# Conditioning vectors of a hybrid decoder step: loaded by input tiles, multiplied 256 columns wide, two more of them in the mixers' waits

## What is computed

```
mod = (silu(c) @ w_ada + b_ada).reshape(B, 9, 1024)      # s1 sc1 g1 s2 sc2 g2 s3 sc3 g3
x = LN(ALPHA*x + 0.5*(1+g1) * swiglu(x*(1+sc1)+s1, ffn1_wgu, ffn1_wdown))
proj = (x*(1+sc2)+s2) @ w_in                             # pooling, RG-LRU and gate inputs
mix  = [pool_mix(u_pool) | gelu(u_gate)*RGLRU(conv(u_lru))] @ w_out
x = LN(ALPHA*x + (1+g2) * mix)
x = LN(ALPHA*x + 0.5*(1+g3) * swiglu(x*(1+sc3)+s3, ffn2_wgu, ffn2_wdown))
```

## Time and profile before

| | |
|---|---|
| median of 3 runs | 1059.66 us (1057.15 to 1059.95) |
| profiled execution | 1059.47 us, of it 1057.5 us span |
| busy share of VectorE, ScalarE, GpSimd | 59%, 43%, 10% |
| moved by the DMA engines | 234.73 MB, mean 222 GB/s |
| conditioning matmuls L511 | 2048 records, mean 274 ns |
| chunks of `ada_raw` | 72 transfers of 1 MiB |

### The profile page before, as it was taken

The page is one execution under the profiler, slowest core; times in us unless marked ns, Lnnn a source line. Parts: engine busy times, 40 slices in busy tenths (PEclk is TensorE's granted clock), DMA queues, the critical chain, the costliest instruction groups (busy, mean ns, idle before and its releaser), DMA issues.

```text
span 1057.5 us, 21707 instructions
## 1 busy us (share of the span) xinstructions
PE 1005.0 (95%) x9548; PEld 970.7 (92%) x9548; DVE 620.1 (59%) x929; ACT 455.3 (43%) x564; POOL 110.5 (10%) x171
## 2 busy tenths in 40 slices
PE   4798999999999999999999999999998989999996
PEld 2598999998988999999989999999897989999995
DVE  1364554457898664544577554455789756555464
ACT  2243443334484444433344444333448445443342
POOL 1420000000510420000006000000060032000000
PEclk9799999999999999999999999999998989999998
DMA  9978898877549679785956998797861627765521
GB/s 302 288 250 235 252 260 299 306 258 235 213 137 275 184 212 273 230 299 176 315 164 216 241 316 238 254 319 255 274 219 51 190 81 205 198 184 158 184 93 42
DMA packets 283329, 234.73 MB, mean 222 GB/s; under 512 B 7328, under 2 KB 249114, under 8 KB 283219
## 3 DMA queue, kind: packets, MB, share of 16 engines
q1 hardware_dynamic: 281136, 229.70, 70.5%
q0 software_dynamic: 1792, 2.54, 0.9%
q10 hardware_dynamic: 306, 1.12, 0.3%
HBM read 232.06 MB, written 1.78 MB: 221 GB/s over the span
## 4 chain that ended last, share of the span: by engine, by line
PE 59%; DVE 7%; DMA 2%; issue 1%; ACT 1%; SPq 0%; DVEq 0%; ACTq 0%
PE bank L485 18%; PE bank L486 18%; PE bank L487 17%; PE bank L511 3%; PE bank L496 2%; DMA raw<-in_ffn_wgu_dram 2%; ACT w_hi L807 1%; DVE w_lo L1019 1%; DVE rstd L1105 1%; DVE xc L1282 1%; DVE z L1095 0%; DVE z L1083 0%; PE bank L692 0%; DVE sq L1109 0%; DVE x L1453 0%
## 5 line engine op out<-in xcount | busy, mean ns | idle before, releaser
L485 PE MATMUL bank<-m_hi,w_hi 128*128 128x264 f32 x1664 | 480.9, 289 | 22.6 <-DVE m_lo L1126 10.7
L486 PE MATMUL bank<-m_lo,w_hi 128*128 128x264 f32 x1664 | 475.9, 286 | 0.0
L487 PE MATMUL bank<-m_hi,w_lo 128*128 128x264 f32 x1664 | 475.1, 286 | 0.0
L1019 DVE TENSOR_TENSOR w_lo<-raw,w_hi 128x2048 fp32r<-128x2048 f32 (+2 forms) x156 | 337.9, 2166 | 223.3 <-ACT w_hi L807 222.7
L807 ACT ACTIVATE w_hi<-raw 128x2048 fp32r<-128x2048 f32 (+2 forms) x156 | 280.1, 1797 | 186.6 <-PE bank L487 165.9
L485 PEld LDWEIGHTS bank<-m_hi,w_hi 128*128 128x128 f32 x1664 | 317.5, 191 | 28.4 <-issue 18.0
L486 PEld LDWEIGHTS bank<-m_lo,w_hi 128*128 128x128 f32 x1664 | 317.8, 191 | 0.1
L487 PEld LDWEIGHTS bank<-m_hi,w_lo 128*128 128x128 f32 x1664 | 316.4, 190 | 0.0
L485 PE MATMUL bank<-h_hi,w_hi 128*128 128x264 f32 x672 | 193.9, 288 | 0.0
L487 PE MATMUL bank<-h_hi,w_lo 128*128 128x264 f32 x672 | 191.0, 284 | 0.0
L486 PE MATMUL bank<-h_lo,w_hi 128*128 128x264 f32 x672 | 190.8, 284 | 0.0
(11 more groups left out here) (208 smaller groups left out, 542.0 us busy)
## 6 DMA issues: line engine op xcount, KB each, us to landing
raw<-in_ffn_wgu_dram SPq DMA_DIRECT2D x168, 512.0 KB, 5.3
ada_raw<-in_w_ada_dram SPq DMA_DIRECT2D x72, 1024.0 KB, 9.8
raw<-in_ffn_wdown_dram SPq DMA_DIRECT2D x48, 512.0 KB, 3.5
raw<-in_ffn_wdown_dram SPq DMA_DIRECT2D x48, 384.0 KB, 4.5
raw<-in_w_in_dram SPq DMA_DIRECT2D x24, 512.0 KB, 4.7
raw<-in_w_out_dram SPq DMA_DIRECT2D x16, 384.0 KB, 4.3
raw<-in_w_out_dram SPq DMA_DIRECT2D x8, 256.0 KB, 4.5
x_rows<-in_x_prompt_dram ACTq DMA_DIRECT2D x1, 1024.0 KB
```

Of the source, the lines that this page charges most:

```text
L485: pe.matmul(out, hi, r_hi, start=start, stop=False)
L486: pe.matmul(out, hi, r_lo, start=False, stop=False)
L487: mm = pe.matmul(out, lo, r_hi, start=False, stop=stop)
L1019: dve.tensor_tensor(w_lo[:, g % SLOTS, 0:n], raw[:, g % SLOTS, 0:n], w_hi[:, g % SLOTS, 0:n].bitcast(F32), ALU.subtract).then_inc(lo_split, 1)
```

## The change

- A chunk holds two input tiles with all 1024 columns of the vector (rows of 4 KiB) instead of four input tiles with half of the columns (rows of 2 KiB).
- A vector is multiplied in matmuls of 256 columns: `vector_half` takes four of the eight input tiles for all columns, so both halves accumulate into one bank, 6 or 7 by the vector's number. There are 32 matmuls (64 records) a vector instead of 64 (128).
- ACT copies a vector once (128x256) instead of twice.
- The two transposes of a vector are replaced by two matmuls with `part` as the weight and `pick`, the nine used columns of four strips of the identity, 36 columns.
- Places: beside units now 2 to 5, 9, 10 and 12 to 14, with new units; 15 takes the wait of 16, 16 is multiplied in layer 1's mixer as 7 is in layer 0's, and 8 and 17 stand behind the mixers' statistics. The filler matmuls and the wait on `part_ready` there are gone, and ACT copies those two vectors behind the high parts of the next phase. DVE finishes them in the up phase's fourth unit.
- The loads stand behind other units (`LOAD_BEHIND`): vector 2 behind unit 4, vector 8 behind 45 and 46, 12 behind 82 and 83, 16 behind 116, 17 behind 123 and 124, and others by a few units.

The hunks left out rename `part` and `ada_raw` views, declare the semaphore, and pass the new names.

```diff
@@ -80,19 +80,13 @@
-    AFTER = {2: (9, 1), 3: (15, 1), 4: (20, 1), 5: (26, 1), 6: (32, 0), 7: (38, 0), 8: (53, 1), 9: (60, 1),
-             10: (68, 1), 11: (77, 0), 12: (85, 1), 13: (92, 1), 14: (98, 1), 15: (104, 1), 16: (110, 0),
-             17: (122, 0)}
-    FIRST_HALF = {AFTER[a][0]: a for a in AFTER if AFTER[a][1]}
-
-    ADA_BANK = {a: (6, 7, 6) for a in range(2, VECTORS)}
-    ADA_BANK[17] = (0, 1, 6)
-
-    LOAD_BEHIND = {2: (5, 6)}
-    for a in range(3, VECTORS):
-        first, apart = AFTER[a - 1]
-        LOAD_BEHIND[a] = (first + 6, first + 6 + apart)
-    LOAD_BEHIND[8], LOAD_BEHIND[17] = (47, 48), (115, 116)
+
+    AFTER = {2: 9, 3: 15, 4: 20, 5: 26, 9: 57, 10: 65, 12: 85, 13: 93, 14: 101}
+    FIRST_HALF = {AFTER[a]: a for a in AFTER}
+
+    LOAD_BEHIND = {2: (4, 4), 3: (15, 16), 4: (21, 22), 5: (26, 27), 6: (32, 33), 7: (38, 38), 8: (45, 46),
+                   9: (50, 51), 10: (63, 64), 11: (71, 72), 12: (82, 83), 13: (91, 92), 14: (99, 100), 15: (107, 108),
+                   16: (116, 116), 17: (123, 124)}
@@ -117,7 +111,7 @@
         w_lo = sb("w_lo", [P, SLOTS, 16 * P], F32R)
-        ada_raw = sb("ada_raw", [P, ADA_SLOTS, DT // 2, D // 2])
+        ada_raw = sb("ada_raw", [P, ADA_SLOTS, 2 * D])
@@ -163,11 +157,12 @@
         rstd = sb("rstd", [P, T])
-        part = sb("part", [P, HALVES, P])
+        part = sb("part", [P, HALVES * P])
         coef = sb("coef", [P, 2, DT, C])
...
         cT = sb("cT", [P, DT, 32])
+        pick = sb("pick", [P, CHUNKS, C])
...
@@ -291,7 +287,7 @@
         out_view = w_out.rearrange("l (k p) d -> l p k d", p=P)
-        ada_view = w_ada.rearrange("l (s k p) (v h d) -> l v h s p k d", s=2, p=P, v=NMOD, h=HALVES)
+        ada_view = w_ada.rearrange("l (j k p) (v d) -> l v j p k d", j=CHUNKS, p=P, v=NMOD)
@@ -332,7 +328,7 @@
                     sync.wait_ge(ada_used, (a - 1) * CHUNKS + c + 1)
-                    sync.dma_start(ada_raw[:, c], ada_view[a // NMOD, a % NMOD, c // 2, c % 2])\
+                    sync.dma_start(ada_raw[:, c].rearrange("p (k d) -> p k d", d=D), ada_view[a // NMOD, a % NMOD, c])\
...
@@ -495,48 +491,48 @@
-            def ada_part(a, h):
-                b = bank[ADA_BANK[a][h]]
+            def vector_half(a, h):
+
+                b = bank[6 + a % 2]
+                if h == 0:
+                    if a < 4:
+                        pe.wait_ge(prep_read, 4)
+                        pe.wait_ge(slice_read, 2 * SLICES)
+                    else:
+                        pe.wait_ge(mod_read, a - 3)
+                for c in (2 * h, 2 * h + 1):
+                    pe.wait_ge(ada_landed[c], (a + 1) * 16)
+                    for k in (2 * c, 2 * c + 1):
+                        for g in range(4):
+                            first = k % 2 * D + g * SLICE
+                            mm = pe.matmul(b[32 * g:32 * g + 32, 0:SLICE], cT[:, k, :],
+                                           ada_raw[:, c, first:first + SLICE], start=k == 0, stop=k == DT - 1,
+                                           tile_position=(0, 32 * g))
+                    mm.then_inc(ada_used, 1)
+
+            def vector_whole(a):
+                vector_half(a, 0)
+                vector_half(a, 1)
+
+            def vector_turn(a):
+
+                pe.wait_ge(part_ready, a - 1)
                 if a == 2:
-                    pe.wait_ge(prep_read, 4)
-                    pe.wait_ge(slice_read, 2 * SLICES)
-                else:
-                    pe.wait_ge(mod_read, a - 2)
-                    pe.wait_ge(part_ready, (a - 3) * HALVES + h + 1)
-                for k in range(DT):
-                    c = 2 * h + k // 4
-                    if k % 4 == 0:
-                        pe.wait_ge(ada_landed[c], (a + 1) * 16)
-                    for g in range(4):
-                        mm = pe.matmul(b[32 * g:32 * g + 32, 0:P], cT[:, k, :],
-                                       ada_raw[:, c, k % 4, g * P:(g + 1) * P], start=k == 0, stop=k == DT - 1,
-                                       tile_position=(0, 32 * g))
-                    if k % 4 == 3:
-                        mm.then_inc(ada_used, 1)
-
-            def ada_turn(a, h):
-                pe.wait_ge(part_ready, (a - 2) * HALVES + h + 1)
-                b = bank[ADA_BANK[a][2]]
-                mm = pe.transpose(b[:, (h + 1) * P:(h + 2) * P], part[:, h], ident[:])
-                if h:
-                    mm.then_inc(mod_out, 1)
-
-            def ada_turns(a):
-                ada_turn(a, 0)
-                ada_turn(a, 1)
+                    pe.wait_ge(pick_ready, 1)
+                b = bank[6 + a % 2]
+                for h in range(HALVES):
+                    mm = pe.matmul(b[:, SLICE + h * 4 * C:SLICE + (h + 1) * 4 * C], part[:, h * P:(h + 1) * P],
+                                   pick[:].rearrange("p g c -> p (g c)"), start=True, stop=True)
+                mm.then_inc(mod_out, 1)
...
                 if g in FIRST_HALF:
-                    ada_part(FIRST_HALF[g], 0)
+                    vector_half(FIRST_HALF[g], 0)
                 if g - 1 in FIRST_HALF:
-                    ada_part(FIRST_HALF[g - 1], 1)
+                    vector_half(FIRST_HALF[g - 1], 1)
                 if g - 2 in FIRST_HALF:
-                    ada_turns(FIRST_HALF[g - 2])
-
-            def keep_warm(b, n):
-                for _ in range(n):
-                    pe.matmul(b[:, 0:P], ident[:], ident[:], start=True, stop=True)
+                    vector_turn(FIRST_HALF[g - 2])
...
@@ -732,18 +728,16 @@
                 gap = vector + 1
-                if l == 0:
-                    ada_part(gap, 0)
-                    ada_part(gap, 1)
+                vector_whole(gap)
...
                     ready(pe, g0 + i)
-                    if i == 1 and l == 0:
-                        ada_turns(gap)
-                    if i == 2 and l == 0:
+                    if i == 1:
+                        vector_turn(gap)
+                    if i == 2:
@@ -760,24 +754,17 @@
                 ffn_stats(l, 0)
-                vector = l * NMOD + (S3, SC3)[l]
-                ada_part(vector, 0)
-                ada_part(vector, 1)
+                vector = l * NMOD + S3
+                vector_whole(vector)
                 mixer(l, vector)
                 mixer_stats(l)
-                if l == 0:
-                    keep_warm(bank[6], 12)
-                else:
-                    ada_part(17, 0)
-                    ada_part(17, 1)
-                    pe.wait_ge(part_ready, (VECTORS - 2) * HALVES)
+                vector_whole(l * NMOD + G3)
                 pe.wait_ge(rows_ready, l + 1)
-                up_phase(l, 1, 17 if l else None)
+                up_phase(l, 1, l * NMOD + G3)
                 down_phase(l, 1)
...
                 if l == 0:
-                    ada_part(11, 0)
-                    ada_part(11, 1)
+                    vector_whole(11)
@@ -806,20 +793,14 @@
-            def ada_copy(a, h):
-                act.wait_ge(ada_used, a * CHUNKS + 2 * h + 2)
-                act.activation(part[:, h], bank[ADA_BANK[a][h]][:, 0:P], ACT.Copy).then_inc(part_ready, 1)
-
-            def ada_copies(a):
-                ada_copy(a, 0)
-                ada_copy(a, 1)
+            def vector_copy(a):
+                act.wait_ge(ada_used, (a + 1) * CHUNKS)
+                act.activation(part[:], bank[6 + a % 2][:, 0:SLICE], ACT.Copy).then_inc(part_ready, 1)
...
-                if g in FIRST_HALF:
-                    ada_copy(FIRST_HALF[g], 0)
                 if g - 1 in FIRST_HALF:
-                    ada_copy(FIRST_HALF[g - 1], 1)
+                    vector_copy(FIRST_HALF[g - 1])
...
@@ -932,8 +913,7 @@
                 split(g0 + 1)
-                if l == 0:
-                    ada_copies(vector + 1)
+                vector_copy(vector + 1)
@@ -951,8 +931,6 @@
                 act.activation(s_rows[0:96], bank[ROWS][0:96, :], ACT.Copy).then_inc(rows_ready, 1)
-                if l:
-                    ada_copies(17)
@@ -977,15 +955,16 @@
                 high(l, 1)
-                mixer(l, l * NMOD + (S3, SC3)[l])
+                mixer(l, l * NMOD + S3)
                 split(l * UNITS + UP[1] + 2)
                 high(l, 2)
+                vector_copy(l * NMOD + G3)
                 up_phase(l, 1)
...
                     high(l + 1, 0)
-                    ada_copies(11)
+                    vector_copy(11)
@@ -1022,9 +1001,10 @@
                 dve.wait_ge(mod_out, a - 1)
-                turned = bank[ADA_BANK[a][2]][:, P:3 * P].rearrange("p (m c) -> p m c", c=32)[:, :, 0:C]
-                dve.tensor_tensor(mod[:, v], turned, bias_mod(l)[:, v].unsqueeze(2).broadcast_to([P, DT, C]),
-                                  ALU.add).then_inc(mod_read, 1)
+                turned = bank[6 + a % 2][:, SLICE:SLICE + DT * C].rearrange("p (h g c) -> p h g c", h=HALVES, c=C)
+                bias = bias_mod(l)[:, v].rearrange("p (g h) -> p h g", h=HALVES)
```

(12 more changed lines are left out.)

17 lines of the change are left out of this document (9 added, 8 removed).

## The result

The kernel after took 1043.49 us in the median (1043.05 to 1044.67), the kernel before 1059.16 beside it: a ratio of 0.9856, with a 95% interval of 0.9841 to 0.987. The forecast was 1045.0. The profiled execution has a span of 1041.0 against 1057.5.

A forecast was written before the change was run, and what follows sets the result against it. TensorE, busy for 95% of the span, was taken as the bound. Terms -8.3 - 0.4 + 4.25 - 4.85 - 6.0 + 0 + 0.6 = -14.7; 1059.5 - 14.7 + 0.2 = 1045.0 us, range 1039 to 1052.

The forecast's parts named there:

- (a): TensorE's stream beside units: two vectors leave it, four halves of 2.08 us each, -8.3 us.
- (b): Vector halves staying in TensorE's stream: 256 columns save 0.02 to 0.03 us a half, -0.4 us in all.
- (c): Turning vectors on TensorE: fourteen matmul turns at 0.55 us replace fifteen transposed ones at 0.23, +4.25 us.
- the bounds: Limits on the turns' cost: -0.2 us if not dearer than a transpose, +9.2 at 0.2 a record.
- (d): Vector 2 loaded behind unit 4: TensorE's 3.15 us wait at unit 7 and 1.7 of clock go, -4.85 us.
- (e): Second mixer's statistics: root no longer held by the vector's copy, 3.82 us plus 2.2 of clock, together -6.0 us.
- clock term: After the second mixer's statistics: TensorE's clock goes back to full, worth 2.2 us.
- (f): Vector 16 in the second mixer's gap: DVE gives the gained clock back, 0 with 1 us either way.
- (g): Loads of vectors 8 and 17 at the mixers' ends: just late, +0.3 us a layer, +0.6.
- rival of late loads: Mixers' ends: vector data at 299 GB/s, 7.0 us per half, +9.8 us, giving 1054.8; chance 0.09.
- 12 to 12.6 from statistics to products: Sign in both mixers: 12 to 12.6 us from the first statistics matmul to the first product.
- 0.67 of a turn: Sign in TensorE's stream: second product 0.67 us after the first of a turn's four records.

The follow-up runs named there:

- Experiment 1: Changed kernel, but a vector is turned by two transposes of 128 columns again instead of two matmuls with pick: 1041.28 us, ratio 0.9825.
- Experiment 3: Changed kernel, but vector 2 is loaded behind units 5 and 6 as before: 1046.16 us, ratio 0.9877.
- experiment 4: Changed kernel, but vector 2 is loaded behind units 5 and 6 and every vector chunk comes in rows of 2 KiB: 1047.55 us, ratio 0.9889.
- experiment 5: Changed kernel, but ACT's copy of vectors 8 and 17 stands ahead of the root of the mixer's statistics in both layers: 1054.13 us, ratio 0.9947.
- experiment 7: Kernel before, plus 14 filler matmuls in layer 1's mixer between the pool matmuls and the output units: 1059.15 us, ratio 0.9994.
- experiment 9: Changed kernel with transposed turns, DVE's split of unit 45 (123) moved behind the coefficients: 1039.54 us with vectors 8 and 17 loaded a unit later, 1040.73 without.

## Why the prediction was right

The time, 1043.49, lies 1.5 under the forecast and inside its range. Step by step:

- **(a), (b) right.** A half costs 2.07 (2.08 less 0.02 predicted). Between the mixers ten halves of 2.07 for fourteen of 2.08 are -8.4, and seven turns of 0.45 for eight of 0.23 are +1.3 (one more turn in each kernel lies in the second mixer's first phase and costs nothing: from its first product to the pool matmuls it is 40.89 before and 40.88 after). That gives -7.1; the ledger has -7.89. Of the difference 0.6 is a short wait of the kernel before that was not in the sum: the 288 products around it took 35.58 us, and the same 288 take 34.98 after. The last 0.2 are not accounted for.
```profile
590.32 0.39 PE L485 MATMUL bank<-m_hi,w_hi 128*128 128x264 f32 x1 [0.32 <-DVE w_lo L1019]
```
- **(c) right in mechanism, too dear.** A turn costs by its records, 0.11 each: 0.45, not 0.55. With the prediction's counts 14 x 0.45 - 15 x 0.23 = +2.85 instead of +4.25. From the first record to the second product after them it is 437.92 - 437.35 = 0.57 here and 0.67 in the row that was taken; that row stands behind an idle 0.53 and not in a stream, which the bounds should have allowed for and the chosen value did not. Experiment 1 also shows that two of the fourteen turns, those inside the mixers' units, cost nothing.
- **(d) right in size, only part of it in cause.** Up to the first mixer -4.26 with four dearer turns (+0.9) in it, so about -5 against -4.85. Experiment 3 shows that the load's place is worth 2.4 with the rest of the change in; the longer rows are worth 0.4 (experiment 4). The remaining 2.3 are, by the traces, 1.1 of shorter wait and, by difference, 1.2 of a clock that no longer falls behind it, and what in the change shortens that wait is not shown. The prediction priced the move against the wait of before and took for granted that the layout left that wait as it was; that the two together come to its figure is luck.
- **(e) right.** The root no longer waits for the vector; undoing it costs 10.9. Its clock term, 2.2, was a little high: in the ledger the stretch behind the second mixer is shorter by 203.79 - 202.01 = 1.78 with a turn in it that is 0.2 dearer, so 2.0. In experiment 5 it is 1.4 and 1.5 after a like idle time; the slow pace lasted 4.3 us in the kernel before and 2.9 and 3.3 there.
- **(f) right in sign, 1 us too high.** Pool matmuls to statistics came to 31.16 and 31.51 instead of 31.9. The reason given, that DVE's one vector more gives the clock back, is not what ends last. Before, the two mixers had nearly the same length for different reasons, the landing of unit 45 in the first and TensorE's low clock in the second (experiment 7), and the prediction read that coincidence as a rule. After, the landing ends last in both; ACT's split begins 22.21 and 22.56 behind the pool matmuls instead of 22.91 and 22.82. What moves the landing by such amounts was not taken apart.
- **(g) the term that was mis-sized upward.** Predicted +0.3 a layer, measured +1.2 and +1.0 (13.36 and 13.10 against 12.14). Unit 46 came 10.07 behind unit 45, not 9.0: half a vector ahead of it cost 6.4 us instead of 5.4 (10.07 - 3.63). In other profiles with the same loads the two layers together lost 1.9 (experiment 1) and 1.0 (experiment 3) instead of 2.2, all more than the 0.6 forecast. The squares, not the products, were what came late. The rival of late loads named this mechanism, with 7.0 a half; the truth lay between, in this profile nearer to it than the forecast.

So (c) was 1.4 too dear and 0.4 for its free turns, the two mixers came 1.1 sooner to their statistics than (f) had it, the unseen wait was 0.6, and (g) was 1.6 too cheap: together 1.9 of the 2.0 by which the ledger's sum fell more than forecast (16.7 against 14.7). Errors of more than 1 us stood on both sides and partly cancelled, so that the time came within 1.5 us is in part luck. Of the signs named beforehand, 12 to 12.6 from statistics to products failed (13.36 and 13.10, by (g)), and so did the 0.67 of a turn (0.57).

## What to carry to other kernels

Cost work in a saturated stream by what the spacing of its neighbours grows, and count records: for small f32 matmuls beside large ones, four records of 36 columns are twice as dear as two of 128 (0.45 against 0.23). A wait for a transfer costs what is queued behind it on the engine that waits, so a load that is put ahead of a unit should be placed by that queue (here squares behind the split of unit 46), not by when the unit itself is used. And when work of one engine is moved out from ahead of one late result, look at once at which result it now stands ahead of: of 2.5 to 3.3 us gained ahead of the statistics 1.8 to 2.2 were given back behind them (experiment 9).
